# Memory and decay rows of a hybrid decoder step: TensorE spreads a column over a row by products with the identity, and VectorE's diagonal products go

## The reference, cut to what matters

```
# group C, one chunk of L=128 positions, per head
b = cumsum(lfc);  a = b + m
dmat = where(causal, b[:,None] - b[None,:] + ic[None,:], -inf)
m_t = maximum(a, max(dmat, -1))
w_in = exp(dmat - m_t[:,None]);  w_st = exp(a - m_t)
s = (q @ k.T) * w_in
h = (s @ v + w_st * (q @ c)) / maximum(abs(den), exp(-m_t))
m_new = m_t[-1]
c = exp(b[-1] + m - m_new) * c + (k * exp(b[-1] - b + ic - m_new)).T @ v

# group D
logits = q @ k.T * scale + cum[q] - cum[k]      # cum = cumsum(logf)
out = softmax(where(causal, logits, -inf)) @ v
```

## Time and profile before

| what | value |
|---|---|
| median of 3 executions | 1773.46 us (1771.76 to 1773.74) |
| profiled execution, its own time | 1777.24 us |
| its span, first to last instruction | 1775.4 us |
| TensorE busy | 1523.5 us, 86% |
| VectorE busy | 625.4 us, 35% |
| ScalarE busy | 317.3 us, 18% |
| mean granted TensorE clock | 0.886 of 2.4 GHz |

### The profile page before, as it was taken

The page is one execution under the profiler, slowest core; times in us unless marked ns, Lnnn a source line. Parts: engine busy times, 40 slices in busy tenths (PEclk is TensorE's granted clock), DMA queues, the critical chain, the costliest instruction groups (busy, mean ns, idle before and its releaser), DMA issues.

```text
span 1775.4 us, 18999 instructions
## 1 busy us (share of the span) xinstructions
PE 1523.5 (86%) x7304; PEld 860.4 (48%) x7304; DVE 625.4 (35%) x1352; ACT 317.3 (18%) x663; POOL 129.5 (7%) x118
## 2 busy tenths in 40 slices
PE   4999998878969849999599999888897993999990
PEld 2455556545544524444244655655655451544440
DVE  1142133764663311111332404456466442111116
ACT  1001012332310101111111000333232010111112
POOL 0000100010000050000200010010000005000002
PEclk9999997787979869999799999877797995999995
DMA  8038443455542459998802302453562324999974
GB/s 290 0 120 240 126 138 114 143 145 128 110 153 72 143 200 343 370 372 324 289 18 72 124 6 83 109 181 120 129 143 76 117 101 183 333 364 367 369 268 172
DMA packets 135949, 317.58 MB, mean 179 GB/s; under 512 B 51396, under 2 KB 81604, under 8 KB 114756
## 3 DMA queue, kind: packets, MB, share of 16 engines
q1 hardware_dynamic: 106688, 187.44, 31.5%
q0 software_dynamic: 12672, 86.51, 15.7%
q10 hardware_dynamic: 16516, 42.63, 6.2%
HBM read 267.35 MB, written 49.19 MB: 178 GB/s over the span
## 4 chain that ended last, share of the span: by engine, by line
PE 62%; issue 16%; DVE 12%; DMA 5%; POOL 2%; ACT 2%; POOLq 0%; SPq 0%; DVEq 0%; ACTq 0%
PE ps L1712 20%; PE ps L2042 7%; PE ps L1998 6%; PE ps L2059 3%; PE ps L1816 3%; DVE ring L1073 3%; PE ps L1715 2%; PE ps L1779 2%; DVE z L1073 2%; DMA kbuf<-in_cache_k,idx_k 2%; PE ps L1761 1%; PE ps L1798 1%; PE ps L1745 1%; DMA ring<-in_w_in 1%; PE ps L1939 1%
## 5 line engine op out<-in xcount | busy, mean ns | idle before, releaser
L1712 PE MATMUL ps<-ring,xT 128*128 128x512 f32 (+1 forms) x896 | 370.9, 574 | 7.5 <-DMA ring<-in_w_in 6.8
L2042 PE MATMUL ps<-ring,z 128*128 128x512 f32 x608 | 272.2, 601 | 1.9 <-ACT z L814 1.9
L1712 PEld LDWEIGHTS ps<-ring,xT 128*128 128x128 f32 x896 | 171.3, 193 | 194.8 <-issue 182.0
L2042 PEld LDWEIGHTS ps<-ring,z 128*128 128x128 f32 x608 | 114.6, 194 | 133.2 <-issue 132.4
L814 ACT ACTIVATE ring<-ps 128x512 f32<-128x512 f32 (+2 forms) x186 | 96.1, 539 | 391.7 <-PE ps L1816 202.3
L814 ACT ACTIVATE z<-ps 128x512 f32<-128x512 f32 (+2 forms) x154 | 79.9, 543 | 454.0 <-PE ps L2042 250.6
L1073 DVE TENSOR_TENSOR z<-ps,vbuf 128x512 f32<-128x512 f32 (+3 forms) x84 | 47.6, 570 | 311.9 <-PE ps L1712 265.9
L2059 PE MATMUL ps<-ring,z 128*128 128x512 f32 x304 | 136.9, 593 | 2.3 <-DVE z L1569 2.3
L1073 DVE TENSOR_TENSOR z<-z,ps 128x256 f32<-128x256 f32 (+1 forms) x40 | 16.5, 412 | 294.7 <-ACT z L814 294.6
L1998 PE MATMUL ps<-ring,xT 128*128 128x512 f32 x256 | 112.0, 595 | 0.0
L1816 PE MATMUL ps<-tab,kbuf 128*128 128x128 f32 x512 | 98.4, 325 | 9.6 <-DMA kbuf<-in_cache_k,idx_k 4.5
(11 more groups left out here) (243 smaller groups left out, 1596.6 us busy)
## 6 DMA issues: line engine op xcount, KB each, us to landing
ring<-in_w SPq DMA_DIRECT2D x114, 1024.0 KB, 8.6
ring<-in_w_in SPq DMA_DIRECT2D x12, 2048.0 KB, 8.7
z<-expert_rows ACTq DMA_DIRECT2D x38, 512.0 KB, 9.0
expert_rows<-z ACTq DMA_DIRECT2D x38, 512.0 KB, 8.5
expert_rows<-zero SPq DMA_DIRECT2D x1, 12288.0 KB, 53.7
ring<-in_w_out SPq DMA_DIRECT2D x4, 2048.0 KB, 11.0
vbuf<-in_b_in SPq DMA_DIRECT2D x2, 1670.0 KB, 15.2
ring<-in_w_in SPq DMA_DIRECT2D x2, 1072.0 KB, 6.0
```

The source lines that it names most:

```text
L1712: m = mm(ps[0:n, i % 4, 0:w], xTv[:, k, t * P:t * P + n], slab[at % 3][:, k, 0:w], start=(k == 0), stop=(k == KD - 1))
L2042: m = mm(ps[:, 2 + s, :].rearrange("p (w f) -> p w f", w=2), xgT[s][:, q, :], w13[s][:, :, q, :], start=(q == 0), stop=(q == KD - 1))
```

## The change

In stage C the column `gp` goes to TensorE itself: for each of the four heads the column, repeated along the free dimension, is the stationary operand and the identity the moving one, so that 128 columns of the row come out of each product. The semaphore `c_dg` now counts twice a tile, once for `gp` and once for the scanned row. The column `mcol` also comes from TensorE: for each head, 128 columns of the scanned row are the stationary operand and one column of the identity the moving one; a new semaphore `c_mc` tells VectorE, which copies the four columns out of PSUM. The copy of `b_t` into `mtb` moves ahead of the scan. In stage D the rows of `ncum` are made likewise, in four products per head, and VectorE only copies. The buffers `diag` and `dg` and the semaphore `d_dg` go.

```diff
-                link(V.scalar_tensor_tensor(gp[0:n], mp[0:n], T("start" + sfx_, n), g_t, ALU.add, ALU.max))
-                tt(diag[0:n, :, 0:n], rep(T("ident", n)[:, 0:n], HEADS), b3(gp[0:n], n), ALU.mult).then_inc(c_dg, 1)
+                V.scalar_tensor_tensor(gp[0:n], mp[0:n], T("start" + sfx_, n), g_t, ALU.add, ALU.max).then_inc(c_dg, 1)
+                V.tensor_copy(mtb[0:n, HEADS:], b_t)
...
-                link(V.tensor_tensor_scan(mr, T("reset" + sfx_, n), ps[0:n, 5, 0:HEADS * n], 0.0, ALU.add, ALU.max))
+                V.tensor_tensor_scan(mr, T("reset" + sfx_, n), ps[0:n, 5, 0:HEADS * n], 0.0, ALU.add, ALU.max).then_inc(c_dg, 1)
+                dve.wait_ge(c_dg, upto(c_dg, 2 * t + 2))
...
-                link(tt(diag[0:n, :, 0:n], rep(T("ident", n)[:, 0:n], HEADS), mr, ALU.mult))
-                link(V.tensor_reduce(mcol[0:n], diag[0:n, :, 0:n], AX.X, ALU.add))
+                dve.wait_ge(c_mc, upto(c_mc, t + 1))
+                link(V.tensor_copy(mcol[0:n], ps[0:n, 5, 0:HEADS]))
                 tt(wx[0:n, 0:HEADS], mp[0:n], mcol[0:n], ALU.subtract)
-                V.tensor_copy(mtb[0:n, HEADS:], b_t)
...
             for h in range(HEADS):
-                if h >= 2:
-                    dve.wait_ge(d_row, upto(d_row, h - 1))
-                tt(dg[h % 2], rep(T("ident"), NP), b3(th(ncum)[:, 0:NP, h:h + 1].rearrange("p t o -> p (t o)"), P), ALU.mult).then_inc(d_dg, 1)
...
+                dve.wait_ge(d_row, upto(d_row, h + 1))
+                V.tensor_copy(ncr[:, h, :], ps[:, 5 + 2 * (h % 2), :]).then_inc(d_ncr, 1)
...
-                pe.wait_ge(c_dg, upto(c_dg, t + 1))
-                m = mm(ps[0:n, 5, 0:HEADS * n], T("ones", n)[:, 0:n], diag[0:n, :, 0:n], start=True, stop=True)
+                pe.wait_ge(c_dg, upto(c_dg, 2 * t + 1))
+                for h in range(HEADS):
+                    m = mm(ps[0:n, 5, h * n:(h + 1) * n], gp[0:n, h:h + 1].to_broadcast([n, n]), idn[0:n, 0:n], start=True, stop=True)
                 m.then_inc(c_row, 1)
                 cache_steps(C_STEPS[0])
                 pe.wait_ge(c_Tsb, upto(c_Tsb, 2 * t + 2))
                 scores(t, c_sc)
                 if t == NP:
                     sample_queries()
+                pe.wait_ge(c_dg, upto(c_dg, 2 * t + 2))
+                for h in range(HEADS):
+                    m = mm(ps[0:n, 5, h:h + 1], mrow_flat[0:n, h * n:(h + 1) * n], idn[0:n, 0:1], start=True, stop=True)
+                m.then_inc(c_mc, 1)
                 cache_steps(C_STEPS[1])
...
             for h in range(HEADS):
-                pe.wait_ge(d_dg, upto(d_dg, h + 1))
                 if h >= 2:
                     pe.wait_ge(d_ncr, upto(d_ncr, h - 1))
-                mm(ps[:, 5 + 2 * (h % 2), :], T("ones"), dg[h % 2].rearrange("p a b -> p (a b)"), start=True, stop=True).then_inc(d_row, 1)
+                for t in range(NP):
+                    c = t * HEADS + h
+                    m = mm(ps[:, 5 + 2 * (h % 2), t * P:(t + 1) * P], ncum[:, c:c + 1].to_broadcast([P, P]), idn, start=True, stop=True)
+                m.then_inc(d_row, 1)
```

More of the change, by code:

```diff
@@ L83 @@
     "d_exp": 16, "d_pTsb": 16, "rms_r": 2, "o_low": 1, "o_rstd": 5, "r_exp": 2, "x_taken": 1, "y_stored": 1,
-    "n_std": 5, "idx_set": 2, "chain_v": 297, "z_sb": 35, "norm_sum": 1, "ws_s8": 1, "va_ready": 1, "rope_done": 1,
+    "n_std": 5, "idx_set": 2, "chain_v": 282, "z_sb": 35, "norm_sum": 1, "ws_s8": 1, "va_ready": 1, "rope_done": 1,
     "f_in": 1, "ws_sb": 2, "f_gates": 1, "gate_sb": 1, "e_tot": 1, "e_cumsb": 1, "b_kd": 5, "b_sw": 5, "b_state": 5,
[L86 to L91, removed]
+    "e_pm": 8, "e_dg": 8, "qm_q": 2, "qm_sb": 2, "e_xs": 8, "km_sb": 8, "e_lf": 8, "e_ym": 8, "c_free": 1, "c_dg": 10,
+    "c_t": 5, "c_mt": 5, "c_gin": 5, "c_kd": 5, "c_sw": 5, "c_cd": 5, "d_ncr": 4, "d_lgx": 16, "d_y": 4, "rms_s": 2,
+    "merged": 2, "m_sb": 10, "y_free": 5, "o_var": 5, "ln_n": 5, "r_lg": 1, "r_e2": 1, "r_picked": 1, "planned": 2,
+    "n_mean": 5, "n_done": 5, "xT_ps": 20, "z_ps": 35, "ws_ps": 2, "gate_ps": 1, "a_ps": 1, "d_cum": 1, "e_T": 1,
+    "e_cumps": 1, "b_T": 5, "e_kps": 64, "b_sc": 5, "e_row": 64, "b_out": 5, "b_up": 4, "e_psum": 8, "e_s": 8,
+    "e_mt": 8, "e_bc": 8, "qm_ps": 2, "km_used": 8, "e_pv": 8, "c_T": 5, "c_row": 5, "c_sc": 5, "c_mc": 5, "c_last": 5,
     "c_out": 5, "c_up": 5, "d_T": 4, "d_row": 4, "d_lg": 16, "d_pT": 16, "d_o": 16, "e_fin": 1, "m_ps": 10, "o_ps": 5,
@@ L290, in decoder @@
         mrow = carve(r2, 2048, HEADS, P)
-        diag = carve(r2, 2560, HEADS, P)
         kd = carve(r2, 3072, GW)
@@ L313, in decoder @@
         lg = [carve(r2, i * SLAB, SEQ) for i in range(2)]
-        dg = [carve(r2, (2 + i) * SLAB, 4, P) for i in range(2)]
         ncr = carve(r2, 2048, HEADS, SEQ)
@@ L475, in decoder @@
         d_cum = sig("d_cum")
-        d_dg = sig("d_dg")
+        c_mc = sig("c_mc")
         d_row = sig("d_row")
@@ L1381, in vector_layer @@
             for h in range(HEADS):
-                if h >= 2:
-                    dve.wait_ge(d_row, upto(d_row, h - 1))
-                tt(dg[h % 2], rep(T("ident"), NP), b3(th(ncum)[:, 0:NP, h:h + 1].rearrange("p t o -> p (t o)"), P), ALU.mult).then_inc(d_dg, 1)
-                if h >= 1:
-                    dve.wait_ge(d_row, upto(d_row, h))
-                    V.tensor_copy(ncr[:, h - 1, :], ps[:, 5 + 2 * ((h - 1) % 2), :]).then_inc(d_ncr, 1)
-            dve.wait_ge(d_row, upto(d_row, HEADS))
-            V.tensor_copy(ncr[:, HEADS - 1, :], ps[:, 5 + 2 * ((HEADS - 1) % 2), :]).then_inc(d_ncr, 1)
+                dve.wait_ge(d_row, upto(d_row, h + 1))
+                V.tensor_copy(ncr[:, h, :], ps[:, 5 + 2 * (h % 2), :]).then_inc(d_ncr, 1)
             dve.wait_ge(d_ncr, upto(d_ncr, HEADS))
```

## The result

| what | before | changed |
|---|---|---|
| first measurement, median | 1772.61 us (4 executions, 1761.31 to 1773.74) | 1797.60 us (4, 1786.54 to 1806.02) |
| its ratio, 95% interval | | 1.0152 [1.0081, 1.0222] |
| second measurement (run e1), median | 1773.99 us (34, 1763.21 to 1794.84) | 1785.23 us (12, 1771.23 to 1810.03) |
| its ratio, 95% interval | | 1.0040 [1.0004, 1.0075] |
| mean of all executions kept | 1774.3 us (106, the befores of runs e1 to e16) | 1787.1 us (14) |

Executions more than 1.5% above the fastest of their kernel in one measurement are left out of the ratios and of the means here (five of twelve for run e5, at most three for any other changed kernel); the medians are over all. The kernel became slower, by 12.8 us or 0.7% on the mean of what was kept.

What follows compares the result with a forecast made beforehand. The prediction took TensorE, 62% of the chain, to bound the kernel. Stage C +1.5 and stage D -0.5 us gave +1.0 per layer, twice +2.0, so the median goes from 1773.46 to 1775.5 us, range 1768.5 to 1781.0.

Steps and rivals of the forecast that it cites:

- its earlier start: Stage C's row: loads begin while transposes stream, gaining 0.2 us in the second tile, 0.75 in the fourth.
- the first three tiles: Stage C: the addition to TensorE's list exceeds the wait it may fill, by +0.48, +0.18 and +0.31 us.
- The column's term: Stage C's column on TensorE: eight loads per tile, 0.97 us at the full clock, 1.78 at the lower.
- the sum: Whole kernel: stage C +1.5 and stage D -0.5 give +1.0 us per layer, twice +2.0; chance 0.6.
- Fourth tile: Stage C: row 0.75 us earlier, column's loads 1.5 near the lower-clock price, together +0.75 us.
- Fifth row to stage D: Stage C's fifth tile: column path 1.85 us against 1.82 today, with 0.24 won, -0.2 (bounds -0.5 and +0.4).
- Stage C as a whole: All five tiles of stage C: +1.5 us per layer, bounds 0.2 and 3.1.
- The rival of the lower clock: Stage C: column made at the lower clock, 0.81 us more per early tile, 2.7 per layer, 1780.9 us; chance 0.2.
- The place where the prediction said it would be wrong: Stage C: the prediction is wrong if the granted clock moves from 0.76 by more than 0.03.
- Stage D: Rows in 4.55 us instead of 5.56; 1.0 less per layer, half taken: -0.5 (bounds 0 and -1.0).
- two signs that I named for the gather: Behind stage D's rows: first layer's wait for the gather of keys longer than 3.55 us, or the landing earlier.
- The bound of 0.2%: Whole kernel: a change under 0.2%, 3.5 us, can hardly be told from none; same got 0.5.

Runs made afterwards that it cites:

- e1: The changed kernel itself, measured and profiled a second time against the kernel before: 1785.23 us, ratio 1.0040.
- e16: Kernel before with stage C and D rows by transposes, column by VectorE, and an unused 512-column product in the fourth tile's pause: 1752.61 us, ratio 0.9867.
- e5: Changed kernel with the column made by four transposes of 128 columns instead of four products: 1778.98 us, 0.9980 of the kernel before.
- e10: Kernel before with four unused products per tile behind the scores, loading like the column's: 1786.93 us, ratio 1.0059.
- e6: Changed kernel with the column made by four transposes of one row each, streaming a single column: 1773.26 us, 0.9968 of the kernel before.
- e11: Kernel before with the rows of stages C and D by TensorE transposes, the column still by VectorE: 1758.05 us, ratio 0.9910.
- e13: Kernel before with an unused 512-column product in the fourth tile's wait for the row: 1766.24 us, ratio 0.9949.
- e15: Changed kernel with rows and column all by transposes, plus an unused 512-column product in the fourth tile: 1771.11 us, 0.9953 of the kernel before.

## Why the prediction was wrong

**The terms of the work held, but for the column's, which was too dear.** The row gained its earlier start (0.26 us in the second tile, 0.2 forecast), and in the fourth tile it started 2.64 us after the transposes instead of 3.37, 0.73 earlier (0.75 forecast). The column's eight loads take 0.97 us in the third tile and 1.78 in the fourth, the two prices that I took from the earlier trace rows. Here the Trainium skill's rule for loads ("TensorE: Matmul & The Clock Gate", "LDWEIGHTS"), which would make them 0.85 at either clock by my estimate from it, is again off by a factor of two at the lower. From the transposes to the last position's values the first three tiles changed by +0.12, -0.12 and -0.10, where I had +0.48, +0.18 and +0.31. At equal lower-level time the parts stand at -4.3 (row), +1.9 (column), -2.3 (stage D) and the whole at -2.4, each within about 1.7 either way, where my terms gave -3.4, +6.4, -1.0 and +2.0. The column's term is off by 4.5 us, and the sign of the sum with it; by this line the work alone would have made the kernel faster.

**The step that failed is the clock at which the sum was made.** I wrote "I count everything twice" and summed each tile at the clock of the kernel before, and let the clock enter only by the price of the added products: 1.5 instead of 0.97 in the fourth tile, 0.81 per tile in the rival. But TensorE's added work moved the clock itself (e10 shows it with loads that nobody waits for), and then all work behind it is dearer, not the added part alone. Fourth tile: +0.75 forecast, +4.87 measured. Fifth row to stage D: -0.2 forecast, +4.13 measured. Stage C as a whole: +1.5 per layer forecast, 3.1 at most, and 6.82 to 8.79 measured in four layers of two profiles. These 15.5 us are the loss that comes each time; that the first profile's 17.8 lie near to them is chance, since the rest of the span moved by +2.3 in it and by -9.4 in the second. The rival of the lower clock named the mechanism but put only 2.7 us per layer on top of the sum's +1.5, 4.2 for stage C, since it priced eight loads and not a tile. The place where the prediction said it would be wrong, a clock in C that moves by more than 0.03, is where it was: 0.50 against 0.81 in the fourth tile, 0.66 against 0.73 behind it, and 0.70 to 0.72 against 0.78 from the first row to stage D's.

**Stage D** went as forecast in the second layer, 4.62 us for the rows (4.55 forecast), and fell short in the first, 5.37, where the products of the third head waited 0.64 us for VectorE's copies. Of the two signs that I named for the gather, a longer wait or an earlier landing, the second came: it landed in 13.10 us instead of 15.41. The run with this part alone has -0.34%, whose interval holds the forecast.

**The base was thin.** Three executions between 1771.76 and 1773.74 suggested a kernel that repeats to 0.1%. Thirty-four executions of it spread from 1763.21 to 1794.84. The bound of 0.2% that my chances rest on needed more executions than the table had.

**What stays open.** Why the fourth tile stays at 1.2 GHz each time when row and column are both changed, and not with either alone (0 of 4 tiles), is not shown: e6 and e11 have it in one layer of two, e11 without any column on TensorE. That filling the pause ends it is shown, and halving the column's loads ended it in both layers of e5 and in one of e6; what in TensorE's list behind the pause decides is not. Nor did I find why the logits of the second layer ran 30 us at the lower level in one execution of the changed kernel, or why the two measurements of this kernel lie so far apart.

## What to carry to other kernels

Work added to TensorE in a stage whose clock goes back and forth is not priced by its own duration: look at the granted clock stretch by stretch and ask of each pause and each rise what the change makes of it, since a clock that doesn't come up makes TensorE's work behind it up to twice as long. Filling a pause is no sure gain: in e13 and e16 the clock fell behind the next wait of the tile, and e15 was no faster for it. A column or row that only has to be moved goes by transposes, not by float32 products with the identity: half the loads and products, 1.2% faster here instead of a loss, three quarters of it at equal lower-level time. And before a forecast of a few us, look at enough executions to know the spread; here the mean clock of each execution went with most of it.

## What the runs showed of the hardware

One product of 1.02 us whose result is thrown away, in a pause of TensorE, shortened a tile from 19.55 to 13.07 us in both layers, and the kernel by 14 to 18 us. Loads that nobody waits for cost 0.5 us at equal clock, but 29 us more at 1.2 GHz and 0.6% of the time. Executions of one and the same kernel differ by some 30 us, and each us more at the lower level goes with 0.36 us of time.
